# Feed-forward and perceptron of a hybrid block: the first product in turned form

## The chip, the cores and the metric

One core of a Trainium2 chip runs the whole kernel. The metric is device microseconds of one execution, the median of several runs. PE is TensorE (its weight loads are PEld), DVE VectorE, ACT ScalarE, POOL GpSimd, SP the queue that issues the loads. Line numbers (L693) are those of the kernel before.

## The reference, cut to what matters

Two blocks follow each other on 256 rows of 1,024 numbers, all in fp32. The first has two layers, each a mixer of three attentions and then a gated feed-forward. The second has two layers, each an attention and then a perceptron with squared ReLU. Only the feed-forward and the perceptron bear on the change:

```
def swiglu(h, w_ffn_in, w_ffn_out):          # twice, FFN_HIDDEN = 2816
    gu = h @ w_ffn_in
    g, u = gu[..., :FFN_HIDDEN], gu[..., FFN_HIDDEN:]
    return (jax.nn.silu(g) * u) @ w_ffn_out

def sq_relu_mlp(x, w_in, w_out):             # twice, D_FF = 4096
    return jnp.square(jax.nn.relu(x @ w_in)) @ w_out
```

Beside the first block's layers runs `mod = silu(c) @ ada_w + ada_b`, whose 12 chunks of 512 columns a layer give the scales and shifts of its norms (the modulation rows).

## The kernel before, in words

**Products in parts.** Every large product is made in fp32r with each operand split in a high part (rounded) and a low part (what is left). A weight unit is 256 rows by 512 columns, 512 KB. SP loads it into one of five raw slots, in one fixed order of all units, rows of constants and modulation weights (`stream`, made by `plan`). ACT rounds it to `hi_units` (L1112, `prep`), POOL subtracts to `lo_units` (L656), five slots each, and PE multiplies (`unit`, L693). A chunk is 512 output columns; its two row tiles of 128 are summed in a pair of PSUM banks, and chunks take the two pairs in turn.

In `unit` the activations are stationary and the weights stream past: for each row tile and each 128 rows of the contraction three passes of 512 columns, high by high, high by low weight, low activation by high weight. A unit is 12 matmuls.

**Activations.** They must lie turned, with the contraction on the partitions, high and low part beside each other (`turned`, and `turned_wide`, called AT, for the hidden numbers). `turn_ffn` (L2076) transposes a finished chunk on PE, 128 by 128 at a time, into the turning banks TQ and TP; ACT copies the rounded part to SBUF (`turn_hi_ffn`, L1140), DVE subtracts the low part (`turn_lo_ffn`, L1489).

**Feed-forward.** Six chunks j of gate (`ffg`) and of value (`ffu`), the last of 256 columns. ACT takes tanh of half the gate from the bank (L1330), DVE makes gate times sigmoid (L1914), then the product with the value into the row buffer `o_rows` (L1922). PE turns chunk j-1 after the gate product of chunk j. The last chunk is turned inside `wide`, the product with `w_ffn_out` over AT.

**Perceptron.** Eight chunks (`mi`). ACT takes ReLU into `mlp_relu` (L1363), DVE squares it, SBUF by SBUF, into `o_rows` (L2058). PE turns chunk j-1 after product j, the last one inside `wide` (product `mo`).

**First chunk.** In both, `beginning` starts chunk 0 while the norm's rows are still being turned: row tile 0 over all four units, then row tile 1.

**Modulation rows.** In the feed-forward of the first layer 32 units of modulation weights are streamed among the weights (three slots), in the second layer 8. DVE multiplies and sums each in two operations (L1431, L1434), rounds and splits a finished chunk (L1439, L1444); PE sums it over the partitions with two matmuls of 512 columns (`ada_sum`, L750, L751), and DVE adds the bias (`ada_drain`, L1455 to L1459). Each engine works its program in order. On DVE `before(key)` does the modulation units that stand in the stream up to one unit past the next chunk, and `after(key)` drains what is complete. PE's `sums()` makes the sums that come due behind a chunk.

Of the kernel before, what the change touches and what calls it, by code (L numbers as in the profile page):

```python
# [29 lines left out]
P = 128  # L30
# [116 lines left out]
def plan():  # L147
# [16 lines left out]

    def vec(name, src, col0, ncols=CW):
# [30 lines left out]
    def phase(parts, adas, summed=True, lead=0, tail=0):  # L196
# [5 lines left out]
        total = sum(-(-args[3] // UNIT_K) for _, args in parts) - lead - tail  # L202
        seen = sent = 0
        for vec_args, args in parts:
            done = []
            c = chunk(*args)
# [25 lines left out]
    for l in range(DEPTH):  # L232
# [31 lines left out]
        for j in range(-(-FFN // CW)):  # L264
            n = min(CW, FFN - j * CW)
            parts.append((None, (("ffg", l, j), ("w_ffn_in", l), 0, KT, j * CW, n)))
            parts.append((None, (("ffu", l, j), ("w_ffn_in", l), 0, KT, FFN + j * CW, n)))
# [8 lines left out]
    for i in range(2):  # L276
# [8 lines left out]
        for j in range(DFF // CW):  # L285
            put(chunk(("mi", i, j), ("mlp_w_in", i), 0, KT, j * CW, CW))
# [38 lines left out]
def program(nc, ctx, dram, out, cat, book):  # L325
# [54 lines left out]
    one_end = union + max(FFN // P * 2 * S * 4 + 2 * NT * CW * 4, NT * (PROJ_W + 3 * D) * 4)  # L380
    MOD, mod_at = place("mod_rows", [P, 6 * D], at=-(-one_end // 64) * 64)
# [174 lines left out]
    def _(sp):  # L556
        sp.dma_start(COND, dram["c"].rearrange("b (p k) -> (b p) k", p=P)).then_inc(c_in, 16)
        sp.dma_start(CON[:, 0:n_early], dram["constants"][:, 0:n_early]).then_inc(const_in, 16)
        for item in stream:
# [32 lines left out]
            else:  # L592
                src, row0, n, col0, ncols = item["src"]
                a = tile_rows(src)[row0:row0 + n * P, col0:col0 + ncols].rearrange("(k p) n -> p k n", p=P)
# [68 lines left out]
    def _(pe):  # L663
        todo = [c for c in chunks]

        def pair_free(c):
            what, i, *half = c["before"]
            if half == [1] and what in ("wo", "mo") or c["before"] == ("ffo", 1, 1):

                pe.wait_ge(vec_used.sem, vec_used.at(("final_g", 1) if what == "ffo" else ({"wo": "ln_mix_b", "mo": "ln_mlp_b"}[what], i, 1)))  # L670
                return
            if c["before"][0] == "mi":
                pe.wait_ge(act_side.sem, act_side.at(("relu", *c["before"][1:])))
            else:
                pe.wait_ge(drained.sem, drained.at(c["before"]))

        def unit(c, i, A, tiles=range(NT)):
# [20 lines left out]
            elif i == len(c["units"]) - 1:  # L698

                ins.then_inc(product.sem, product.mark(("first tile", c["key"])))  # L700

# [97 lines left out]
        def wide(tag, n, name, following):  # L799

            c = todo.pop(0)
            last = n - 1
            width = (FFN - last * CW if name == "ffo" else CW) // P
            for i in range(len(c["units"])):
                if i == 2 * last - 2:
                    turn_ffn(pe, turned, turned_lo, rows, drained, tag, last, width, BANK, TQ, TP, O, con)

                pe.wait_ge(turned_lo.sem, turned_lo.at((tag, i // 2, 1)))
# [125 lines left out]
        for l in range(DEPTH):  # L934
# [93 lines left out]
            n_ff = -(-FFN // CW)  # L1028
            for j in range(n_ff):
                if j < n_ff:  # L1030
                    for what in ("ffg", "ffu"):
                        if (what, j) != ("ffg", 0):
                            c = todo.pop(0)
                            assert c["key"] == (what, l, j)
                            for i in range(len(c["units"])):
                                unit(c, i, HT)
                        sums()
                        if what == "ffg" and j:
                            turn_ffn(pe, turned, turned_lo, rows, drained, ("a", l), j - 1, min(CW, FFN - (j - 1) * CW) // P, BANK, TQ, TP, O, con)
            wide(("a", l), n_ff, "ffo", (("n1", 1), O, n1_rows) if l + 1 < DEPTH else (("x", 0), X, x_rows(0)))  # L1040
        for i in range(2):
# [17 lines left out]
            for j in range(DFF // CW):  # L1059
                if j:  # L1060
                    c = todo.pop(0)
                    for u in range(len(c["units"])):
                        unit(c, u, HT)
                    turn_ffn(pe, turned, turned_lo, rows, drained, ("a2", i), j - 1, CW // P, BANK, TQ, TP, O, con)
            wide(("a2", i), DFF // CW, "mo", (("x", 1), X, x_rows(1)) if i == 0 else None)
# [1050 lines left out]
```

## Time and profile before

| | |
|---|---|
| median of 3 runs | 1515.95 us (1514.25 to 1517.46) |
| profiled execution: time, span | 1513.58 us, 1511.8 us |
| busy of the span | PE 97%, PEld 81%, POOL 81%, DVE 47%, ACT 47% |
| instructions | 20,262, of them 7,242 matmuls |
| HBM read | 311.39 MB |

A busy share says how long an engine had something in hand, not that it set the end; which engine does is read from the chain that ended last. Matmuls are pipelined, so the time of one is read from how often they start, not from its own duration.

### The profile page before, as it was taken

Reading aid. Unit: us, or ns where it says so; the run is one execution under the profiler, and the core shown is the slowest. Engines: PE = TensorE matmul, PEld = TensorE weight load, DVE = VectorE, ACT = ScalarE, POOL = GpSimd, SP = SyncE. Lnnn points to the kernel's source line nnn. Section 1 sums busy time; section 2 is a strip of 40 time slices with the busy share of each in tenths; the row PEclk is TensorE's granted clock in tenths of the full one; section 3 lists DMA queues with packets and bytes.
Section 4 is the critical chain, followed back from the end, with each engine's and each line's share of the span. In section 5 each row is a group of like instructions: output and inputs, shape, how many; then the busy total and the mean of one; then the engine's idle time right before and its main releaser. Section 6 shows DMA issues by size and latency. Waiting matters only on the chain.

```text
span 1511.8 us, 20262 instructions
## 1 busy us (share of the span) xinstructions
PE 1473.0 (97%) x7242; PEld 1220.8 (81%) x7242; DVE 710.6 (47%) x1398; ACT 711.8 (47%) x1074; POOL 1217.6 (81%) x984
## 2 busy tenths in 40 slices
PE   7999999999999999999999999999999999999997
PEld 3898887788888987888788887778888888788886
DVE  7577655665724668656433114264331053643212
ACT  3345554544444344545544445465554345455432
POOL 4799989798797976548898888908999977389994
PEclk9999999999999999999999999999999999999999
DMA  9995546799976985426676665715655656166553
GB/s 356 317 391 178 176 157 190 232 354 304 299 230 207 380 269 153 133 84 214 197 245 187 198 219 162 212 56 153 195 185 191 211 166 208 46 177 195 182 188 104
DMA packets 168238, 313.79 MB, mean 208 GB/s; under 512 B 11061, under 2 KB 36041, under 8 KB 168137
## 3 DMA queue, kind: packets, MB, share of 16 engines
q1 hardware_dynamic: 166384, 311.15, 64.0%
q10 hardware_dynamic: 1754, 1.35, 0.3%
q8 instruction: 58, 0.95, 0.3%
q14 instruction: 42, 0.34, 0.1%
HBM read 311.39 MB, written 1.06 MB: 207 GB/s over the span
## 4 chain that ended last, share of the span: by engine, by line
PE 86%; DVE 5%; POOL 3%; DMA 3%; ACT 2%; issue 1%; SPq 0%; DVEq 0%; ACTq 0%; POOLq 0%
PE bank L693 75%; POOL lo_units L656 3%; PE bank L2076 2%; PE bank L838 2%; PE bank L859 1%; DMA raw_units<-in_w_in 1%; ACT hi_units L1112 1%; PE bank L827 1%; PE bank L826 1%; PE bank L877 1%; PE bank L825 1%; DMA row_vectors<-in_norm_g 1%; DMA raw_units<-in_w_out 1%; PE bank L725 1%; PE bank L862 0%
## 5 line engine op out<-in xcount | busy, mean ns | idle before, releaser
L656 POOL TENSOR_TENSOR lo_units<-raw_units,hi_units 128x512 fp32r<-128x512 f32 (+3 forms) x944 | 1167.7, 1275 | 258.9 <-ACT hi_units L1112 257.3
L693 PE MATMUL bank<-hi_units,turned 128*128 128x512 f32 (+2 forms) x2688 | 832.6, 385 | 4.6 <-POOL lo_units L656 3.0
L1112 ACT ACTIVATE hi_units<-raw_units 128x1024 fp32r<-128x1024 f32 (+3 forms) x478 | 485.5, 1018 | 535.4 <-PE bank L693 428.4
L693 PEld LDWEIGHTS bank<-hi_units,turned 128*128 128x128 f32 x2688 | 501.6, 189 | 98.9 <-POOL lo_units L656 4.3
L693 PE MATMUL bank<-lo_units,turned 128*128 128x512 f32 (+3 forms) x1344 | 511.6, 381 | 0.0
L693 PE MATMUL bank<-hi_units,turned_wide 128*128 128x512 f32 x992 | 311.0, 391 | 0.9 <-DVE turned_wide L1482 0.9
L693 PEld LDWEIGHTS bank<-lo_units,turned 128*128 128x128 f32 x1344 | 253.8, 189 | 41.9 <-issue 0.2
L693 PEld LDWEIGHTS bank<-hi_units,turned_wide 128*128 128x128 f32 x992 | 186.2, 188 | 39.9 <-DVE turned_wide L1482 1.1
L693 PE MATMUL bank<-lo_units,turned_wide 128*128 128x512 f32 x496 | 193.1, 389 | 0.0
L1434 DVE SCALAR_TENSOR_TENSOR bank<-ada_units,small,bank 128x512 f32<-128x512 f32 x144 | 108.8, 756 | 54.0 <-DMA ada_units<-in_ada_w 49.7
L693 PEld LDWEIGHTS bank<-lo_units,turned_wide 128*128 128x128 f32 x496 | 93.2, 188 | 19.0 <-issue 0.2
L2058 DVE TENSOR_TENSOR o_rows<-mlp_relu 128x512 f32<-128x512 f32 x32 | 47.1, 1510 | 116.2 <-ACT mlp_relu L1363 116.2
L1489 DVE TENSOR_TENSOR turned_wide<-bank,turned_wide 128x512 fp32r<-128x512 f32 (+1 forms) x56 | 37.7, 672 | 93.2 <-ACT turned_wide L1140 91.4
L1227 ACT ACTIVATE scores<-scores,small 128x128 f32<-128x128 f32 x60 | 24.0, 400 | 57.8 <-DVE small L1649 57.2
L1914 DVE SCALAR_TENSOR_TENSOR ffn_tanh<-ffn_tanh,bank 128x512 f32<-128x512 f32 (+1 forms) x24 | 14.3, 639 | 70.1 <-ACT ffn_tanh L1330 70.0
L1951 DVE SCALAR_TENSOR_TENSOR bank<-x_rows,bank 128x512 f32<-128x512 f32 x8 | 5.6, 696 | 75.8 <-PE bank L693 75.6
L838 PE MATMUL bank<-constants,scores 128*128 128x128 f32 x180 | 31.1, 282 | 4.9 <-DVE o_rows L1667 1.9
L693 PE MATMUL bank<-hi_units,branch_turned 128*128 128x512 f32 x96 | 32.8, 403 | 0.0
L1667 DVE TENSOR_TENSOR o_rows<-bank,small 128x128 f32<-128x128 f32 x48 | 14.0, 292 | 37.6 <-PE bank L827 36.6
L1922 DVE SCALAR_TENSOR_TENSOR o_rows<-ffn_tanh,bank 128x512 f32<-128x512 f32 (+1 forms) x24 | 14.3, 639 | 35.0 <-PE bank L693 34.9
L1146 ACT ACTIVATE turned<-bank 128x512 fp32r<-128x512 f32 x28 | 16.8, 599 | 27.7 <-PE bank L725 27.7
L1229 ACT ACTIVATE scores<-scores,small 128x256 f32<-128x256 f32 x60 | 29.7, 494 | 0.0
(235 smaller groups left out, 1238.1 us busy)
## 6 DMA issues: line engine op xcount, KB each, us to landing
ada_units<-in_ada_w SPq DMA_DIRECT2D x88, 512.0 KB, 7.6
raw_units<-in_w_ffn_in SPq DMA_DIRECT2D x80, 512.0 KB, 4.5
raw_units<-in_mlp_w_in SPq DMA_DIRECT2D x64, 512.0 KB, 4.0
raw_units<-in_mlp_w_out SPq DMA_DIRECT2D x64, 512.0 KB, 3.3
raw_units<-in_w_in SPq DMA_DIRECT2D x56, 458.0 KB, 7.6
raw_units<-in_w_in SPq DMA_DIRECT2D x48, 512.0 KB, 3.9
raw_units<-in_w_ffn_out SPq DMA_DIRECT2D x44, 512.0 KB, 4.1
raw_units<-in_moba_w_qkv SPq DMA_DIRECT2D x24, 512.0 KB, 4.1
```

Source lines behind the costliest of these rows:

```text
L656: pool.tensor_tensor(LO[:, s, b, 0:w], RAW[:, u["slot"], b, 0:w], HI_[:, s, b, 0:w].bitcast(F32), ALU.subtract).then_inc(lo_ready.sem, lo_ ...
L693: ins = pe.matmul(BANK[2 * c["pair"] + t][:, 0:w], xs[:, part, :], W[:, s, b, 0:w], start=(i == 0 and m == 0 and q == 0), stop=(i == len(c ...
L725: ins = pe.transpose(BANK[(TQ, TP)[n % 2]][:, j * P:(j + 1) * P], src[:, t, (4 * half + j) * P:(4 * half + j + 1) * P], con("ident"))
L838: ins = pe.transpose(bank[:, at:at + P], SM[:, h % N_SM, cols], con("ident"))
L1112: act.activation(HI_[:, s, 0:n, 0:w], RAW[:, u["slot"], 0:n, 0:w], ACT.Copy)\
L1146: act.activation(A[:, 4 * half:4 * half + 4, 0, t * P:(t + 1) * P], BANK[(TQ, TP)[n % 2]][:, :].rearrange("p (k s) -> p k s", k=4), ACT.Copy)\
L1227: act.activation(SM[:, h % N_SM, S:S + P], SM[:, h % N_SM, S:S + P], ACT.Exp, bias=NM[:, m:m + 1], scale=-1.0, accum_out=RS[:, m:m + 1])
L1229: act.activation(SM[:, h % N_SM, 0:S], SM[:, h % N_SM, 0:S], ACT.Exp, bias=NM[:, m + 1:m + 2], scale=-1.0, accum_out=RS[:, m + 1:m + 2]).t ...
L1434: ins = v.scalar_tensor_tensor(total, raw[:, k, :], COND[:, kt:kt + 1], partial, ALU.mult, ALU.add)
L1489: tell(v.tensor_tensor(AT[:, 4 * j:4 * j + n, 1, t * P:(t + 1) * P], BANK[(TQ, TP)[t]][:, 0:n * P].rearrange("p (k s) -> p k s", k=n), AT[ ...
L2058: ins = v.tensor_tensor(O[:, t, (j % 2) * CW:(j % 2 + 1) * CW], RT[:, j % 2, t, :], RT[:, j % 2, t, :], ALU.mult)
L2076: ins = pe.transpose(BANK[(TQ, TP)[t]][:, k * P:(k + 1) * P], O[:, t, (j % 2) * CW + k * P:(j % 2) * CW + (k + 1) * P], con("ident"))
```

## The change

Chunk 0 of gate and value, and chunk 0 of the perceptron, stay as they are. All later hidden columns are made in tiles of 128 columns in turned form: the weights are stationary and the activations stream past, high and low part side by side in 512 columns, then the low weight over the 256 columns of the high activations. What comes out has the hidden columns on the partitions, and its two halves of 256 have to be added. A unit is now the 1,024 rows of one tile; the weights come from copies laid out in such tiles (`w_ffn_tiles`, `mlp_w_tiles`, made before the launch), 4 KB in a row. A feed-forward has 18 such tiles of gate and value (36 units, keys `fft`), a perceptron 28 tiles (two in a chunk, keys `mit`).

DVE adds the two halves (`both_parts`, a reduction over a view with stride 256) from the product's bank into the first 256 columns of a turning bank. Gate, tanh, ReLU, square and the splitting then work there and write AT directly. Only chunk 0 is transposed, between the two units of the first turned chunk. The plan spreads the modulation units over 2 units a turned chunk. The core of the diff:

```
+        def tile_free(c, i):
+            what, l, n = c["before"]
+            if what == "mit":
+                pe.wait_ge(rows.sem, rows.at(("sum", l, n + i)))
+            elif what == "fft" and i == 0:
+                pe.wait_ge(rows.sem, rows.at(("gate tile", l, n)))
+            elif what == "fft":
+                pe.wait_ge(drained.sem, drained.at(c["before"]))
+            elif i == 0:
+                pair_free(c)
+
+        def turned_unit(c, i, A):
+            u = c["units"][i]
+            tile_free(c, i)
+            s = u["index"] % NH
+            bank = BANK[2 * c["pair"] + i]
+            for kt in range(KT):
+                b, at = divmod(kt * P, CW)
+                if at == 0:
+                    pe.wait_ge(lo_ready.sem, lo_ready.at((u["index"], b)))
+                pe.matmul(bank[:, :], HI_[:, s, b, at:at + P], A[:, kt, :, :].rearrange("p two s -> p (two s)"), start=kt == 0, stop=False)
+                ins = pe.matmul(bank[:, 0:S], LO[:, s, b, at:at + P], A[:, kt, 0, :], start=False, stop=kt == KT - 1)
+            ins.then_inc(unit_used.sem, unit_used.mark(u["index"]))
+
+        def turned_product(key, between=None):
+            c = todo.pop(0)
+            turned_unit(c, 0, HT)
+            if between:
+                between()
+            turned_unit(c, 1, HT)
...
-                pe.wait_ge(turned_lo.sem, turned_lo.at((tag, i // 2, 1)))
+                pe.wait_ge(turned_lo.sem, turned_lo.at((tag, 0, 1) if i < CW // P // 2 else (tag, "tile", 2 * i + 1)))
                 unit(c, i, AT)
...
+            for n in range(CW // P, FFN // P):
+                turned_product(("fft", l, n), first_turn if n == CW // P else None)
+                sums()
...
+            for n in range(CW // P, DFF // P, 2):
+                turned_product(("mit", i, n), first_turn if n == CW // P else None)
```

ACT, in the feed-forward and in the perceptron:

```
+        def hidden_hi(tag, n, h):
+            act.wait_ge(rows.sem, rows.at((tag, "hidden", n)))
+            act.activation(AT[:, n, 0, :], h, ACT.Copy).then_inc(turned_hi.sem, turned_hi.mark((tag, "hidden", n)))
...
+            for n in range(CW // P, FFN // P):
+                prep_chunk(("fft", l, n), NH - 1)
+                if n == CW // P:
+                    turn_hi_ffn(("a", l), 0, CW // P)
+                act.wait_ge(rows.sem, rows.at(("gate tile", l, n)))
+                act.activation(TGN[:, n % 2, 0, :], BANK[TQ][:, 0:S], ACT.Tanh, scale=0.5)\
+                    .then_inc(act_side.sem, act_side.mark(("tg", l, n)))
+                prep_chunk(("fft", l, n))
+                hidden_hi(("a", l), n, BANK[TP][:, 0:S])
...
+                for m in (n, n + 1):
+                    act.wait_ge(rows.sem, rows.at(("sum", i, m)))
+                    act.activation(RTN[:, m % 4, :], BANK[(TQ, TP)[m % 2]][:, 0:S], ACT.Relu).then_inc(act_side.sem, act_side.mark(("relu tile", i, m)))
+                    prep_chunk(("mit", i, n), NH - 1 if m == n else NH)
+                    hidden_hi(("a2", i), m, BANK[(TQ, TP)[m % 2]][:, 0:S])
```

DVE, in the same order:

```
+        def hidden_lo(tag, n, h):
+            dve.wait_ge(turned_hi.sem, turned_hi.at((tag, "hidden", n)))
+            tell(v.tensor_tensor(AT[:, n, 1, :], h, AT[:, n, 0, :].bitcast(F32), ALU.subtract), turned_lo, (tag, "tile", n))
+
+        def both_parts(to, bank):
+            return v.tensor_reduce(to, bank[:, :].rearrange("p (two s) -> p s two", two=2), AX_X, ALU.add)
...
+            for n in range(CW // P, FFN // P):
+                key = ("fft", l, n)
+                tg, g, u = TGN[:, n % 2, 0, :], BANK[TQ][:, 0:S], BANK[TP][:, 0:S]
+                if n == CW // P:
+                    turn_lo_ffn(("a", l), 0, CW // P)
+                say(both_parts(g, tile_product(dve, key, 0)), ("gate tile", l, n))
+                if n > CW // P:
+                    hidden_lo(("a", l), n - 1, u)
+                if n < FFN // P - 1:
+                    before(key)
+                dve.wait_ge(act_side.sem, act_side.at(("tg", l, n)))
+                link(v.scalar_tensor_tensor(tg, tg, 1.0, g, ALU.add, ALU.mult))
+                tell(both_parts(u, tile_product(dve, key, 1)), drained, key)
+                say(v.scalar_tensor_tensor(u, tg, 0.5, u, ALU.mult, ALU.mult), (("a", l), "hidden", n))
+                after(key)
...
+                for m in (n, n + 1):
+                    h = BANK[(TQ, TP)[m % 2]][:, 0:S]
+                    if m == CW // P:
+                        turn_lo_ffn(("a2", i), 0, CW // P)
+                    say(both_parts(h, tile_product(dve, key, m - n)), ("sum", i, m))
+                    if m > CW // P:
+                        hidden_lo(("a2", i), m - 1, BANK[(TQ, TP)[(m - 1) % 2]][:, 0:S])
+                    dve.wait_ge(act_side.sem, act_side.at(("relu tile", i, m)))
+                    say(v.tensor_tensor(h, RTN[:, m % 4, :], h, ALU.mult), (("a2", i), "hidden", m))
```

`tile_product` waits for one unit and gives its bank; TGN and RTN are 256-column views of the tanh and ReLU buffers.

## Rows read from the trace of the kernel before

**Rows 1.** The page: busy shares, the chain's shares, products of L693 (group rows).

```profile
PE 1473.0 (97%) x7242; PEld 1220.8 (81%) x7242; DVE 710.6 (47%) x1398; ACT 711.8 (47%) x1074; POOL 1217.6 (81%) x984
...
PE 86%; DVE 5%; POOL 3%; DMA 3%; ACT 2%; issue 1%; SPq 0%; DVEq 0%; ACTq 0%; POOLq 0%
PE bank L693 75%; POOL lo_units L656 3%; PE bank L2076 2%; PE bank L838 2%; PE bank L859 1%; DMA raw_units<-in_w_in 1%; ACT hi_units L1112 1%; PE bank L827 1%; PE bank L826 1%; PE bank L877 1%; PE bank L825 1%; DMA row_vectors<-in_norm_g 1%; DMA raw_units<-in_w_out 1%; PE bank L725 1%; PE bank L862 0%
...
L693 PE MATMUL bank<-hi_units,turned 128*128 128x512 f32 (+2 forms) x2688 | 832.6, 385 | 4.6 <-POOL lo_units L656 3.0
...
L693 PEld LDWEIGHTS bank<-hi_units,turned 128*128 128x128 f32 x2688 | 501.6, 189 | 98.9 <-POOL lo_units L656 4.3
```

**Rows 2.** Chain in order of time, first perceptron: start us, us, what.

```profile
1060.41 0.87 PE bank L2076 x8
1061.29 10.90 PE bank L693 x48
1072.19 0.87 PE bank L2076 x8
...
1131.93 32.66 PE bank L693 x144
```

**Rows 3.** The same view, first feed-forward.

```profile
289.60 27.25 PE bank L693 x120
316.85 0.23 PE bank L750
...
405.98 5.75 PE bank L693 x48
...
434.00 0.44 PE bank L2076 x4
```

**Rows 4.** Timeline of ACT and DVE around chunk 0: start us, us, instruction.

```profile
306.09 1.28 DVE L1922 SCALAR_TENSOR_TENSOR o_rows<-ffn_tanh,bank 128x512 f32<-128x512 f32 x2 [1.40 <-PE bank L693]
...
1049.63 1.06 ACT L1112 ACTIVATE hi_units<-raw_units 128x1024 fp32r<-128x1024 f32 x1 [0.30 <-PE bank L693]
1050.60 1.07 ACT L1363 ACTIVATE mlp_relu<-bank 128x512 f32<-128x512 f32 x2
...
1051.77 3.45 DVE L2058 TENSOR_TENSOR o_rows<-mlp_relu 128x512 f32<-128x512 f32 x2 [6.29 <-ACT mlp_relu L1363]
...
1074.41 2.61 DVE L2058 TENSOR_TENSOR o_rows<-mlp_relu 128x512 f32<-128x512 f32 x2 [6.85 <-ACT mlp_relu L1363]
...
1335.48 3.45 DVE L2058 TENSOR_TENSOR o_rows<-mlp_relu 128x512 f32<-128x512 f32 x2 [6.33 <-ACT mlp_relu L1363]
```

**Rows 5.** Timeline of POOL, end of the first perceptron's chunks.

```profile
1120.52 2.99 POOL L656 TENSOR_TENSOR lo_units<-raw_units,hi_units 128x512 fp32r<-128x512 f32 x2 [0.19 <-ACT hi_units L1112]
...
1144.06 2.54 POOL L656 TENSOR_TENSOR lo_units<-raw_units,hi_units 128x512 fp32r<-128x512 f32 x2 [0.18 <-ACT hi_units L1112]
```

**Rows 6.** Busy time in one stretch, first feed-forward: us, engines, PEclk, DMA, GB/s.

```profile
289.00:412.00 123.00, 123.00 (x611) 104.29 (x610) 80.29 (x114) 58.63 (x71) 107.92 (x93) 1.00 0.92 311
```

**Rows 7.** Groups by form on DVE in the same stretch, modulation rows.

```profile
L1434 DVE SCALAR_TENSOR_TENSOR bank<-ada_units,small,bank 128x512 f32<-128x512 f32 x51 | 38.5, 756 | 7.8 <-DMA ada_units<-in_ada_w 6.1
...
L1459 DVE SCALAR_TENSOR_TENSOR mod_rows<-bank,row_vectors 128x512 f32<-128x512 f32 x2 | 1.4, 692 | 0.1
```

**Rows 8.** Groups by form, whole span, DVE and ACT.

```profile
L1504 DVE TENSOR_TENSOR bank<-x_rows,mod_rows 128x512 f32<-128x512 f32 x6 | 6.8, 1175 | 0.1
...
L1953 DVE BATCH_NORM_STATS2 small<-bank 128x6 f32<-128x512 f32 x8 | 5.6, 699 | 0.3
...
L1489 DVE TENSOR_TENSOR turned_wide<-bank,turned_wide 128x256 fp32r<-128x256 f32 x4 | 1.7, 426 | 33.4 <-ACT turned_wide L1140 33.3
...
L1112 ACT ACTIVATE hi_units<-raw_units 128x1024 fp32r<-128x1024 f32 x382 | 404.0, 1059 | 407.1 <-PE bank L693 383.9 <-DMA raw_units<-in_w_out 7.9 <-DMA raw_units<-in_w_ffn_out 7.5
...
L1140 ACT ACTIVATE turned_wide<-bank 128x256 fp32r<-128x256 f32 x4 | 1.3, 370 | 0.0
```

**Rows 9.** Waits in the first feed-forward: us in total, times, longest us.

```profile
ACT hi_units L1112 <- DMA raw_units<-in_w_ffn_in: 2.4, 1, 2.4
```

More of the change, by code:

```diff
@@ L163, in chunk, with tile_chunk @@
         return c
+    def tile_chunk(key, tiles):
+        c = dict(key=key, kind="gemm", pair=pair[0] % 2, ncols=CW, units=[])
+        pair[0] += 1
+        for name, l, n in tiles:
+            c["units"].append(dict(kind="w", index=count["w"], n=UNIT_K, ncols=CW, src=("tiles", name, l, n)))
+            count["w"] += 1
+        chunks.append(c)
+        return c
     def vec(name, src, col0, ncols=CW):
@@ L201, in phase @@
         made = {}
-        total = sum(-(-args[3] // UNIT_K) for _, args in parts) - lead - tail
+        total = sum(2 if args[0][0] == "fft" else -(-args[3] // UNIT_K) for _, args in parts) - lead - tail
         seen = sent = 0
@@ L671, in pair_free @@
                 return
+            if what == "mit":
+                pe.wait_ge(rows.sem, rows.at(("sum", i, half[0] + 1)))
+                return
             if c["before"][0] == "mi":
@@ L1027, in _ @@
             beginning(("n2", l), O, n2_rows, HT)
[L1028 to L1040, printed above, removed]
+            c = todo.pop(0)
+            assert c["key"] == ("ffu", l, 0)
+            for i in range(len(c["units"])):
+                unit(c, i, HT)
+            sums()
+            first_turn = lambda l=l: turn_ffn(pe, turned, turned_lo, rows, drained, ("a", l), 0, CW // P, BANK, TQ, TP, O, con)
+            for n in range(CW // P, FFN // P):
+                turned_product(("fft", l, n), first_turn if n == CW // P else None)
+                sums()
+            wide(("a", l), (("n1", 1), O, n1_rows) if l + 1 < DEPTH else (("x", 0), X, x_rows(0)))
         for i in range(2):
@@ L1058, in _ @@
             beginning(("m", i), X, m_rows, HT)
[L1059 to L1065, printed above, removed]
+            first_turn = lambda i=i: turn_ffn(pe, turned, turned_lo, rows, drained, ("a2", i), 0, CW // P, BANK, TQ, TP, O, con)
+            for n in range(CW // P, DFF // P, 2):
+                turned_product(("mit", i, n), first_turn if n == CW // P else None)
+            wide(("a2", i), (("x", 1), X, x_rows(1)) if i == 0 else None)
         assert not todo
@@ L1925, in _ @@
[L1925 removed]
+            kg, ku = ("ffg", l, 0), ("ffu", l, 0)
+            before(kg)
+            banks = product_ready(dve, kg)
+            dve.wait_ge(act_side.sem, act_side.at(("tg", l, 0)))
+            for t in range(NT):
+                ins = v.scalar_tensor_tensor(TG[:, 0, t, :], TG[:, 0, t, :], 1.0, banks[t][:, :], ALU.add, ALU.mult)
+            tell(ins, drained, kg)
+            after(kg)
+            before(ku)
+            banks = product_ready(dve, ku)
@@ L2101, in traced, with in_tiles @@
     return nc
+def in_tiles(inputs):
+    out = {}
+    for name, to in (("w_ffn_in", "w_ffn_tiles"), ("mlp_w_in_2", "mlp_w_tiles_2")):
+        w = np.asarray(inputs[name])
+        tiles = w.reshape(w.shape[0], KT, P, -1, P).transpose(0, 3, 2, 1, 4)
+        out[f"in_{to}"] = np.ascontiguousarray(tiles).reshape(w.shape[0], -1, P, D)
+    return out
 def kernel(**inputs):
```

125 lines of the change are left out of this document (51 added, 74 removed).

## The prediction

> **What bounds the kernel now.** I read the page's busy shares first: PE holds 97% of the span and nothing else comes near except POOL at 81% [rows 1]. The chain that ended last confirms that this is work and not a coincidence of busy engines: PE carries 86% of it, the products of L693 alone 75%, and the transposes of L2076 2% [rows 1]. So time falls only if PE streams less or waits less, and any other engine costs nothing until it makes PE wait. I then read the chain in order of time, in one perceptron [rows 2] and in the first feed-forward [rows 3]: product, transposes, product, with no gap between them. Four units take 10.90 us, a group of eight transposes 0.87 us. The granted clock is full in these stretches (1.00, that is 2.4 GHz, in the first feed-forward [rows 6]), so I take durations as they stand.
>
> **Part 1, the transposes that go.** A perceptron has eight groups of eight transposes; seven go. The group takes 0.87 us [rows 2], so 2 x 7 x 0.87 = 12.2 us. A feed-forward has five groups of eight and one of four (0.44 us [rows 3]); four of eight and the one of four go: 2 x (4 x 0.87 + 0.44) = 7.8 us. They lie on the chain itself, so all 20.0 us come off PE.
>
> **Part 2, the product in turned form.** A unit was 12 matmuls of 512 columns: 10.90 / 4 = 2.725 us, or 227 ns for one with its weight load beside it. It becomes 8 matmuls of 512 and 8 of 256 columns, the same 6,144 columns in 16 pieces. For a 256-column one there is a row: the half-width chunk of the feed-forward, 48 in 5.75 us, 120 ns each, every one with a 128-column load of its own [rows 3]. So a turned unit costs 8 x 0.227 + 8 x 0.120 = 2.775 us. Perceptron: 28 units a layer, 28 x 0.05 = 1.4 us more. Feed-forward: before, 32 full units and 8 half ones (5.75 / 4 = 1.44 us), 87.2 + 11.5 = 98.7 us; after, 36 x 2.775 = 99.9, 1.2 us more. Both layers of both: +5.2 us. Bounds: without the extra four fixed parts (227 ns less 213 ns of columns, 14 ns each) it would be +0.0 to +0.5; from above, a load's own record lasts 189 ns [rows 1]; if a short matmul couldn't run under it, each of the 1,024 short ones would take 69 ns more, 70 us in all. The half-width chunk has the same loads (loads and matmuls stand in equal numbers) and runs at 120 ns, so I keep 120 and leave that end to rival D. The rule that speaks for that end is the Trainium skill's "TensorE: Matmul & The Clock Gate", section "LDWEIGHTS (loading the stationary operand)": a load takes its columns over 1.2 GHz, by estimate 107 ns for 128, what 256 columns take at 2.4 GHz, so nothing would be to spare. By that rule the trace agrees in the half-width chunk, 107 ns of columns and 120 ns measured, so the sum would be the same.
>
> **Part 3, the turn of the first chunk moves forward.** Only chunk 0 is still transposed, and now between the two units of the first turned product, one unit (2.775 us) after chunk 0 ends; before, a whole chunk (10.9 us) lay between. What must be ready is the squares or the gated rows in the row buffer.
> In the perceptron ACT's conversion at 1049.63 starts as chunk 0's last unit ends (about 1049.5); ReLU runs from 1050.60 and the two squares of L2058 from 1051.77 to 1055.22 [rows 4]. So the rows are ready 5.8 us after the chunk, and PE, with 2.775 us of work, stands 3.0 us; the other perceptron shows the same 3.45 us pair [rows 4]. 2 x 3.0 = +6.0 us. Queued behind the wait are the transposes and all later units; ACT's next conversions wait behind the turn too, but they have about four units (11 us) of lead. Bounds: the same pair took 2.61 us once [rows 4], so 2 x 2.2 = 4.4; above, 7.5 if ACT is late by another conversion (1.06 us less a semaphore). The pair is this slow against 1.28 us for a gating pair [rows 4] since both its inputs lie in SBUF while POOL reads there too: POOL's unit takes 2.99 us beside it and 2.54 us otherwise [rows 5]. The new operations all have an input in PSUM, as the gating pair has, so I charge POOL nothing for them.
> In the feed-forward DVE's gating of chunk 0 ran 306.09 to 307.37 [rows 4], 1.4 us after the chunk ended near 305.95: inside one unit, no stall.
>
> **Part 4, what DVE, ACT and POOL get.** Per turned tile of 128 hidden columns. DVE: a sum of two halves of a bank. No such reduction stands in the trace; it reads 512 elements of PSUM, and its nearest rows, statistics over a bank and the drain of one, take 0.69 to 0.70 us [rows 7, 8]. I take 0.69. Lower bound 0.43 us (a 256-element operation, since it writes 256 [rows 8]); upper 1.18 us, the slowest 512-element form that touches PSUM [rows 8]. Low part, gate and product over 256 go by the low part of the old half chunk, 0.42 us each [rows 8].
> Perceptron, per unit of 2.775 us: DVE 0.69 + 2 x 0.42 = 1.5 us; ACT one conversion 1.06 and two 256-wide passes of 0.37 [rows 8], 1.8 us; POOL 2.54 us [rows 5]. All fit, hidden by PE's 2.775 us; POOL has the least to spare, 0.23 us, and were it slower by more than that, PE would follow it (2.85 us a unit would be 56 x 0.075 = 4 us). Against that, in the wide products PE already runs 144 matmuls in 32.66 us, 2.72 a unit, over the same POOL work [rows 2].
> The first feed-forward is the tight one. DVE has the modulation rows there: 59.7 us for 29.5 of its units in 123 us (seven rows, the first and the last shown) [rows 7], 2.02 us each, 2.1 with gaps. By the plan 27 of 32 are streamed by the end of the turned tiles, 4 are done before, so 23: 48.7 us. Gating and splitting 18 tiles: 18 x (2 x 0.69 + 3 x 0.42 + gaps 0.18) = 50.7 us. First turn 1.4 and waiting for it 2.5. Together 103.3 us. PE in the same stretch: 99.9 + 0.87 + six modulation sums of 0.46 [rows 3] = 103.5 us. DVE is as full as PE. What softens it: PE needs a sum only two tiles later (three units, 8.3 us) and a finished modulation row about 5 us after DVE can start it. So a lag under 5 us is free. I charge 1.0 us; bounds 0 and, with the sum at 1.18 us, 36 x 0.49 - 5 = 12.6 us. In the second feed-forward only 8 modulation units come: nothing.
> DMA moves the same bytes, in rows of 4 KB in place of 2 KB; the queue's weights landed in time (ACT waited 2.4 us for them in that stretch, once [rows 9], and PE didn't wait: busy 123 of 123 us [rows 6]). 0. The moved place of the next waits (the wide product needs tile 5 at its third unit, the last tile at its last) is far behind the work: 0.
>
> **Sum.** -20.0 + 5.2 + 6.0 + 1.0 = -7.8 us. On the profiled execution: 1513.6 (span 1511.8) to 1505.8. The median shown is 2.4 us above that execution, so 1515.95 - 7.8 = 1508.1, 0.5% faster. A measurement here tells about 0.2%, 3.0 us.
>
> **Rivals.**
> A. The stalls are small: pairs of squares at 2.61 us and no loss on DVE: -20.0 + 5.2 + 4.4 = -10.4, 1505.6. For it: the 2.61 us pair. Against: both first pairs took 3.45.
> B. DVE's lag in the first feed-forward grows beyond its 5 us, by in-order waits for tanh and for modulation transfers (DVE waited 6.1 us for the latter in this stretch before [rows 7]): 4 to 8 us lost, -5 to -1, 1511 to 1515. Against: each look-ahead for transfers is now shorter, two units in place of four.
> C. The other side: the sum over the halves takes about 1.2 us. DVE then needs 36 x 0.49 = 17.6 us more in the first feed-forward, 12.6 beyond the lag: -20.0 + 5.2 + 6.0 + 12.6 = +3.8, 1519.7. It decides from 0.69 + (8.8 + 5) / 36 = 1.07 us per sum. For it: the 1.18 us row, and no row of a reduction. Against: every form with one PSUM input and no second SBUF input takes 0.69 to 0.76 us.
> D. Short matmuls bound by their loads: 70 us at the full 69 ns, 1578; it decides the sign from 8 ns each (1,024 x 0.008 = 8 us). The half-width row speaks against it.
>
> **Chances.** Forecast (1506.5 to 1510) 0.50, A and anything better 0.18, B 0.18, C 0.10, D 0.04. Faster by over 0.2% (below 1512.9): forecast, A and a third of B, 0.74. Within 0.2%: the rest of B and a little of C, 0.14. Slower: 0.12. The range leaves out D, half of C and the best of A: 1503.5 to 1518.
>
> **What would show it.** Right: four turned units of one stage 11.1 us apart on the chain; 32 transposes of L2076's kind in place of 216; PE idle 3 us in the first turned product of each perceptron, released by the squares; reductions at 0.69 us; POOL at 2.54 us a unit all through the perceptron. Wrong: PE waiting in the first feed-forward for DVE's sums or its modulation rows; a sum over 1 us; 256-column matmuls more than 120 ns apart; POOL over 2.77 us a unit, which would make it the bound.

## The result, and the profile after

The changed kernel takes 1523.28 us (median of 6 runs, 1520.28 to 1525.83) against 1515.47 us (1513.47 to 1517.46, 6 runs) before: ratio 1.0049, interval [1.0034, 1.0065]. It is slower by 7.8 us where 7.8 us less were forecast. The profiled execution took 1525.83 us (span 1524.0), the slowest of the six, so its span stands 12.2 us above that of before and not 7.8.

The page after (busy shares, then the chain's shares by engine):

```profile
PE 1470.8 (97%) x7474; PEld 1225.8 (80%) x7474; DVE 798.1 (52%) x1630; ACT 718.1 (47%) x1154; POOL 1206.8 (79%) x968
...
PE 73%; DMA 7%; DVE 7%; POOL 7%; ACT 3%; issue 1%; SPq 0%; DVEq 0%; ACTq 0%
```

PE's share of the chain fell from 86% to 73%, while its busy share stayed at 97% [rows 1]. Most of the 13% went to DMA, POOL and DVE: somewhere the kernel waits for them. To see where, I cut both traces at the last four transposes that turn a norm's output, which stand at the head of each stage (us from there to the next, or to the end):

| stage | before | after | difference |
|---|---|---|---|
| first feed-forward | 191.5 | 200.3 | +8.8 |
| attention of layer 2 | 248.9 | 249.2 | +0.3 |
| second feed-forward | 189.5 | 188.7 | -0.8 |
| first perceptron | 184.2 | 186.8 | +2.7 |
| second perceptron | 184.7 | 184.3 | -0.3 |

The rest of the 12.2 us is 1.4 us ahead of the first feed-forward and 0.2 us in the two attentions of the second block, where the code is the same. No changed stage gained what its transposes took (3.9 or 6.1 us), and one lost 9.

**New operations.** Groups by form, whole span (count, busy us, mean ns, idle before):

```profile
L746 PE MATMUL bank<-turned,hi_units 128*128 128x512 f32 x1024 | 363.6, 400 | 0.2 <-DVE bank L1557 0.2
...
L747 PE MATMUL bank<-turned,lo_units 128*128 128x256 f32 x1024 | 287.7, 281 | 0.0
...
L1557 DVE TENSOR_REDUCE bank<-bank 128x256 f32<-128x512 f32 x128 | 89.5, 700 | 94.9 <-PE bank L747 93.3
```

The sum over two halves takes 700 ns, for which 0.69 had been taken. A matmul's own duration overlaps the next; its true cost is read from the starts, in the next view.

**First perceptron, chain in order of time.**

```profile
1059.23 1.06 ACT hi_units L1165
1060.29 0.98 ACT mlp_relu L1416 x2
...
1061.36 3.44 DVE o_rows L2128 x2
...
1064.84 1.97 PE bank L2155 x8
1066.81 0.43 PE bank L746
1067.24 0.21 PE bank L747
1067.45 0.43 PE bank L746
...
1071.90 0.24 PE bank L746
...
1072.96 0.24 PE bank L746
```

Conversion, ReLU, squares, then the transposes, as foreseen, with PE idle 2.9 us. Not foreseen is what follows: the eight transposes take 1.97 us where 0.87 is usual [rows 2], and a long and a short matmul take 0.64 us (1066.81 to 1067.45). From 1071.90 on three pairs take 1.06 us, 0.353 each. The windows over PE (us busy, granted clock, DMA share, GB/s) say why:

```profile
1060.00:1064.00 4.00, 1.94 (x12) 1.00 0.75 249
1064.00:1068.00 4.00, 3.16 (x13) 0.52 0.41 135
1068.00:1072.00 4.00, 4.00 (x17) 0.63 0.37 131
1351.00:1355.00 4.00, 3.49 (x15) 0.59 0.48 142
```

Behind the wait the granted clock stands at 0.50, the 1.2 GHz level, until 1071.0; some 6 us of PE's work fall in it. The fourth row is the same place in the second perceptron, where the low stretch is half as long. Its length isn't given by the stall: with the same early turn the low stretch behind it in the first perceptron is as long in e4_mlp_only (6.9 us), and half as long (3.4 us) in e2_half_mod, e3_grouped and e11_paced_only.

The pace of a pair is not one number either. From the second perceptron, on the same chain:

```profile
1385.11 0.23 PE bank L746
...
1386.15 0.23 PE bank L746
```

Three pairs take 1.04 us, 0.347 each, at the same clock of 1.00. So the units of the second perceptron start 2.77 us apart, while those of the second feed-forward and the first perceptron start 2.83 us apart. As long as units follow each other without an interruption they keep one of the two paces; behind a wait or a modulation sum it can change, as it does within the first feed-forward.

**First feed-forward, one stretch** (columns as in [rows 6]), and under it the waits in it, of the engines and then of SP's queue (us in total, times, longest). The last fence has the queue's waits for DVE in the same stretch of the kernel before:

```profile
300.00:425.00 125.00, 121.29 (x665) 103.93 (x664) 103.88 (x167) 54.80 (x80) 104.35 (x84) 1.00 0.83 290
```

```profile
ACT hi_units L1165 <- DMA raw_units<-in_w_ffn_tiles: 35.1, 18, 4.7
...
DVE ffn_tanh L1996 <- ACT ffn_tanh L1390: 7.3, 6, 3.1
```

```profile
SPq L604 <- DVE bank L1491: 46.2, 15, 8.6
SPq L604 <- DVE sum_low L1501: 28.7, 6, 7.5
SPq L619 <- POOL lo_units L674: 11.2, 13, 2.2
```

```profile
SPq L591 <- DVE sum_low L1444: 7.1, 5, 2.5
SPq L591 <- DVE bank L1434: 2.6, 4, 1.7
```

PE is no longer busy throughout. ACT, which waited once for weights before [rows 9], waits 18 times, 35.1 us. Yet the DMA engines are busy only 0.83 of the time (0.92 before [rows 6]): the transfers are issued late. SP issues them in one fixed order, and now stands 75 us (9.7 before) at L604, a modulation load, until DVE frees one of the three slots; every weight load behind it in the queue stands too. The chain shows a whole turn of this, at the end of the tiles:

```profile
415.99 5.30 DMA raw_units<-in_w_ffn_out
...
421.32 0.03 ACT hi_units L1165
...
422.28 0.38 ACT turned_wide L1199
...
422.75 0.44 DVE turned_wide L1553
...
425.52 0.70 DVE sum_low L1501
...
426.24 0.37 SPq L604
...
426.65 6.08 DMA raw_units<-in_w_ffn_out
...
432.76 1.07 ACT hi_units L1165
...
433.89 2.52 POOL lo_units L674 x2
...
436.45 14.68 PE bank L714 x57
```

Weights land late; ACT's small pass on the hidden tile is queued behind their conversion; DVE waits for that pass, with the modulation unit queued behind; the slot is freed late; SP issues the next weights 10 us after the last ones. This is a ring of waits: each step is late by the one before it, and the last one makes the first late again. The start of the output product pays for it: in the tiles PE is idle 3.7 us, behind them another 3, with a stretch at the lower clock.

### The profile page after: what moved, and what is told of

The parts are those of the page before. It is cut to its first block, busy times and chain, and to the rows that moved or that the text cites. A ratio compares the mean times of both kernels' runs of the same rounds, so it can differ in the third digit from the quotient of the medians.

```text
span 1524.0 us, 21278 instructions
## 1 busy us (share of the span) xinstructions
PE 1470.8 (97%) x7474; PEld 1225.8 (80%) x7474; DVE 798.1 (52%) x1630; ACT 718.1 (47%) x1154; POOL 1206.8 (79%) x968
## 3 DMA queue, kind: packets, MB, share of 16 engines
HBM read 311.39 MB, written 1.06 MB: 205 GB/s over the span
## 4 chain that ended last, share of the span: by engine, by line
PE 73%; DMA 7%; DVE 7%; POOL 7%; ACT 3%; issue 1%; SPq 0%; DVEq 0%; ACTq 0%
PE bank L714 47%; PE bank L746 11%; POOL lo_units L674 7%; PE bank L747 6%; DMA ada_units<-in_ada_w 3%; DMA raw_units<-in_w_ffn_tiles 2%; PE bank L891 1%; ACT hi_units L1165 1%; PE bank L912 1%; DVE bank L1491 1%; DMA raw_units<-in_w_ffn_out 1%; DMA raw_units<-in_w_in 1%; PE bank L880 1%; PE bank L879 1%; PE bank L930 1%
## 5 line engine op out<-in xcount | busy, mean ns | idle before, releaser
L1165 ACT ACTIVATE hi_units<-raw_units 128x1024 fp32r<-128x1024 f32 (+1 forms) x470 | 483.2, 1031 | 431.1 <-PE bank L714 225.0
L714 PE MATMUL bank<-hi_units,turned 128*128 128x512 f32 (+3 forms) x1600 | 508.3, 389 | 4.6 <-POOL lo_units L674 3.0
L746 PE MATMUL bank<-turned,hi_units 128*128 128x512 f32 x1024 | 363.6, 400 | 0.2 <-DVE bank L1557 0.2
L714 PEld LDWEIGHTS bank<-hi_units,turned 128*128 128x128 f32 x1600 | 301.4, 189 | 62.1 <-POOL lo_units L674 4.3
L714 PE MATMUL bank<-lo_units,turned 128*128 128x512 f32 (+3 forms) x800 | 306.7, 383 | 0.0
L747 PE MATMUL bank<-turned,lo_units 128*128 128x256 f32 x1024 | 287.7, 281 | 0.0
L746 PEld LDWEIGHTS bank<-turned,hi_units 128*128 128x128 f32 x1024 | 193.6, 189 | 47.6 <-DVE bank L1557 0.5
L747 PEld LDWEIGHTS bank<-turned,lo_units 128*128 128x128 f32 x1024 | 194.5, 190 | 0.5
L714 PEld LDWEIGHTS bank<-lo_units,turned 128*128 128x128 f32 x800 | 151.5, 189 | 23.9 <-issue 0.2
L1557 DVE TENSOR_REDUCE bank<-bank 128x256 f32<-128x512 f32 x128 | 89.5, 700 | 94.9 <-PE bank L747 93.3
```

The source lines that it names most:

```text
L714: ins = pe.matmul(BANK[2 * c["pair"] + t][:, 0:w], xs[:, part, :], W[:, s, b, 0:w], start=(i == 0 and m == 0 and q == 0), stop=(i == len(c ...
L746: pe.matmul(bank[:, :], HI_[:, s, b, at:at + P], A[:, kt, :, :].rearrange("p two s -> p (two s)"), start=kt == 0, stop=False)
L747: ins = pe.matmul(bank[:, 0:S], LO[:, s, b, at:at + P], A[:, kt, 0, :], start=False, stop=kt == KT - 1)
L1165: act.activation(HI_[:, s, 0:n, 0:w], RAW[:, u["slot"], 0:n, 0:w], ACT.Copy)\
L1557: return v.tensor_reduce(to, bank[:, :].rearrange("p (two s) -> p s two", two=2), AX_X, ALU.add)
```

## The experiments

Stage times are those of the profiled execution of each kernel; medians are over all its runs. Each kernel was timed beside runs of the kernel before, whose median was 1515.3 to 1516.2 us throughout.

**1. The turn behind both units of the first turned chunk, in the perceptrons alone** (e1_late_turn).

```
             turned_unit(c, 0, HT)
-            if between:
+            if between and not late:          # late: the perceptrons
                 between()
             turned_unit(c, 1, HT)
+            if between and late:
+                between()
```

> The changed kernel, only that in the two perceptrons the turn of chunk 0 comes after both units of the first turned chunk, not between them. Theory: PE stands about 3 us in each perceptron for the squares, and in the first one its clock then falls (matmul pairs 640 ns apart for about 3 us), so two units (5.65 us) under a wait of 5.8 us leave 0.2 us: 6 to 9 us less than the changed kernel (1523.3), 1514 to 1517. Rival: the perceptron is paced by POOL or by DVE's sums, and the wait only moves: within 1.5 us of 1523.3.

1516.09 us, ratio 1.0002 [0.9991, 1.0012], 7.2 us less than the changed kernel; the perceptrons take 181.2 and 180.3 us in place of 186.8 and 184.3. Its chain at the same place:

```profile
1059.81 3.48 DVE o_rows L2131 x2
...
1063.33 1.09 PE bank L2158 x8
1064.43 0.23 PE bank L746
```

**2. PE kept at work through the wait** (e8_filled): the changed kernel with 12 matmuls, read by nobody, between the first unit and the turn.

> The changed kernel, with 12 matmuls of 512 columns, whose product nobody reads, between the first turned unit and the turn of each perceptron's first chunk: 12 x 227 ns = 2.7 us, so that TensorE works through the wait for the squares instead of standing idle. It saves no waiting. Theory (the idle 2.9 us is followed by a stretch at the lower clock, which costs 3.4 us in the first perceptron and 1 to 2 in the second): the granted clock stays at 1.00 behind the turn, the eight transposes take 0.9 us, the pairs 353 ns, and the kernel 3 to 5 us less than the changed one, 1518 to 1520. Rival (the clock falls for another reason, or the stretch is slow because the bank's readers are in the way): transposes still take 2 us, pairs 640 ns, and the time stays at 1523.

1520.87 us (10 runs), ratio 1.0034 [1.0022, 1.0045]: 2.4 us less than the changed kernel, just short of the 3 to 5 expected. The perceptrons take 184.0 and 183.1 us. The windows over PE:

```profile
1064.00:1068.00 4.00, 3.86 (x25) 1.00 0.52 150
1068.00:1072.00 4.00, 4.00 (x25) 1.00 0.29 113
```

The clock stays full although the wait is as long. So the stall of 2.9 us had two prices in the profiled execution: itself, and 2.8 us (first perceptron) and 1.2 us (second) at the low clock. The Trainium skill, "TensorE: Matmul & The Clock Gate", section "What's actually happening", says that the clock's gate follows how busy the array has recently been; by that rule the trace agrees.

The second price isn't paid each time. In e11_paced_only (below), with the same early turn, the second perceptron has the same stall (2.9 us idle in these two rows) and no fall:

```profile
1334.00:1338.00 4.00, 1.42 (x9) 1.00 0.60 215
1338.00:1342.00 4.00, 3.70 (x24) 1.00 0.51 161
```

That fits the medians, where keeping PE at work gave 2.4 us and not 4.0. What decides whether the clock falls behind a wait of this length, and for how long, no run here shows.

**3. Long matmuls first, then the short ones** (e3_grouped, on the changed kernel; e6_late_grouped, on e1_late_turn).

```
             for kt in range(KT):
                 (long matmul)
+            for kt in range(KT):
                 (short matmul)
```

> The changed kernel, each turned unit with its eight 512-column matmuls first and its eight 256-column ones behind them. In the changed kernel a pair takes 353 ns where rows of equal length give 227 + 120 = 347. Theory: the change of length after each matmul costs the 6 ns, and grouping takes 128 x 8 x 6 ns = 6 us off PE; of it 3 to 4 us are seen (the first feed-forward waits for DVE anyway): 1519 to 1521. Rival: the operands' places cost it, whatever the order: within 1.5 us of 1523.3.

> Late turn as in e1_late_turn, and the eight long matmuls of a turned unit ahead of its eight short ones. Theory (a part of the 353 ns that a pair takes, above 227 + 120, comes from the alternation of lengths): a unit takes 2.78 to 2.80 us in place of 2.83, the second feed-forward 187.2 us in place of 188.2, each perceptron 1 us less than in e1_late_turn, so 1512 to 1514. Rival (it belongs to the lengths, not to their order): 1516, as e1_late_turn.

e3_grouped: 1522.2 us, ratio 1.0041 [1.0025, 1.0057]; e6_late_grouped: 1515.22 us, 0.9989 [0.9979, 1.0000]. Each is about 1 us below its base, within the intervals, and above the range expected of it; the 1522.2 us lie in the rival's range. The starts of the units say more. Grouped units start 2.79 us apart in all four stages of both kernels, wherever nothing comes between. Alternating ones start 2.83 or 2.77 us apart, so grouping gains where they held the slower pace (second feed-forward 187.4 us against 188.7 in the changed kernel; first perceptron 180.4 against 181.2 in e1_late_turn) and loses where they held the faster one (second perceptron 180.8 against 180.3). So the 6 ns above 227 + 120 belong to the alternation, but only to one of its two paces; at the other it costs nothing. Why there are two is open.

**4. The first feed-forward apart.** e4_mlp_only has both feed-forwards as before the change and the perceptrons as after it.

> Both feed-forwards as before the change, both perceptrons as after it. By the stages of the two traces the feed-forwards account for 8.0 us of the loss (8.8 in the first, -0.8 in the second) and the perceptrons for 2.3 us (2.6 and -0.3). Theory: 1516 to 1518. Rival, the loss lies in the perceptrons: 1521 to 1524.

1517.46 us, 1.0007 [0.9995, 1.0018], first feed-forward back at 191.5 us. e7_first_ffn_old has only the first one as before, with late turn and grouped matmuls in the rest.

> Late turn, grouped matmuls, and the first feed-forward as before the change; the second feed-forward and both perceptrons in turned form. Theory: stages of 191.5 us (first feed-forward, as before the change), 187.2 (second), 180.5 and 179.5 (perceptrons), which is 2 + 3.7 + 5.2 us less than before the change in the three changed stages: 1503 to 1508. Rival (what the second feed-forward and the perceptrons save is only moved to a later wait): 1512 to 1516.

1505.14 us (5 runs), ratio 0.9932 [0.9917, 0.9947]; stages 191.5, 187.4, 180.4 and 180.8 us. The turned form is worth its transposes in three stages of four.

**5. Less work on DVE.** e2_half_mod is the changed kernel without the second multiplication of each modulation unit in the first feed-forward (these sums are half left out). e5_three_short keeps all work, but spares DVE the sum over halves.

```
-    (long: W_hi x [A_hi A_lo] -> bank[:, 0:512]), (short: W_lo x A_hi -> bank[:, 0:256])
+    (short: W_hi x A_hi), (short: W_hi x A_lo), (short: W_lo x A_hi), all -> bank[:, 0:256]
```

> The changed kernel, but DVE leaves out the second of the two multiplications of every modulation unit streamed in the first layer's feed-forward (half of those sums is missing from the result); all transfers stay. DVE gets about 18 us lighter there, DMA stays as it is. Theory: DVE is overfull in that stage and holds back both the modulation slots, behind which the weights queue, and the tanh and split steps: PE's waits there go, about 9 us less than the changed kernel, 1513 to 1516. Rival: the transfers themselves are too slow (HBM rate, 4 KB rows): within 1.5 us of 1523.3.

> The turn of the perceptron's first chunk stands behind both units, as in e1_late_turn. Besides, in the first feed-forward alone each pair of a long and a short matmul becomes three short ones into columns 0 to 255 of the bank, so that VectorE copies 256 numbers where it had to add two halves (700 ns each, 36 of them in that stage). Theory (VectorE is overfull in the first feed-forward and its lateness reaches TensorE through the slots of the modulation's raw columns): VectorE gets back some 10 us there, at 0.35 to 0.4 us less for each of 36 sums 12 to 14 us, while TensorE pays 8 x (3 x 120 - 353) ns = 0.06 us a unit, about 2 us in all; the stage comes from 199.9 us to 193 to 196, the whole to 1508 to 1513. Rival (the transfers of that stage are late by themselves, since tile by tile weights come in another order): the stage stays at 199 to 202 us and the whole at 1516 to 1519.

e2_half_mod: 1517.68 us, 1.0013 [1.0000, 1.0026], 5.6 less than the changed kernel (about 9 expected), stage 192.7. e5_three_short: 1510.77 us, 0.9970 [0.9961, 0.9979], within its range, but its stage took 198.7, above the 193 to 196 expected. The window over the tiles, of e2_half_mod and then of e5_three_short:

```profile
300.00:425.00 125.00, 125.00 (x685) 107.67 (x684) 88.25 (x146) 56.44 (x82) 108.16 (x87) 1.00 0.84 301
```

```profile
300.00:425.00 125.00, 125.00 (x964) 121.41 (x963) 97.29 (x172) 54.39 (x79) 106.06 (x85) 1.00 0.82 290
```

In both PE works through, with every transfer where it was, so DVE has a part in the loss within the tiles, and the bytes alone don't make it. But e5_three_short still lost 3.2 us at the start of the output product, and the clock fell there. The theory as I had it, DVE simply overfull, was not enough.

**6. The same work, transfers spread wider.** The plan places one modulation unit for each 1.5 weight units. Here a turned tile's unit counts 0.7 (e9_paced) or 0.8 (e10_paced_08) and the last ones of the output product count too, so that 24 or 25 of 32 are streamed by the end of the tiles and not 27.

```
-                seen += 1
+                seen += share if args[0][0] == "fft" else 1
```

> All four stages in turned form, late turn and grouped matmuls as in e6_late_grouped. Besides, the plan spreads the 32 modulation units of the first feed-forward otherwise: a unit of a turned tile counts 0.7 and not 1, and the last half unit of the first output product counts too, so that 23 and no longer 27 of them are streamed by the end of the tiles; the rest lies beside the output product. Nothing is left out. Theory (VectorE is overfull in the tiles, and four modulation units less are 4 x 2.1 = 8.4 us of its 103): TensorE no longer waits there, the stage takes 190 to 194 us in place of 201.7, the whole 1504 to 1508. Rival (the first transfers of the output product's weights are late anyway, as in e5_three_short, where VectorE had 10 us less and the stage still took 198.6 us): 196 to 199 us, the whole 1510 to 1513.

> As e9_paced with 0.8 in place of 0.7: 25 of the 32 modulation units by the end of the tiles. Theory: VectorE has 4.2 us less, half of what e9_paced gives, so the stage takes 194 to 198 us and the whole 1508 to 1511; were it the same as e9_paced, VectorE's fullness would not be what counts but the place of the transfers. Rival: no change to e6_late_grouped, 1515.

e9_paced: 1506.39 us, 0.9933 [0.9910, 0.9956], stage 192.0. e10_paced_08: 1505.36 us, 0.9926 [0.9905, 0.9947], stage 191.3, better than expected. (The expectation counts 23 units for e9_paced; in the order in which SP issues them it is 24, counted as the 27 and the 25 are.) Two units moved out of 27 gave back all of the 10 us, and three gave no more. By its expectation that speaks against DVE's load and for the place of the transfers. The waits of e10_paced_08 in the stretch 300:425:

```profile
SPq L604 <- DVE bank L1496: 52.9, 17, 7.6
SPq L604 <- DVE sum_low L1506: 23.7, 7, 5.7
```

```profile
ACT hi_units L1170 <- DMA raw_units<-in_w_ffn_tiles: 21.0, 10, 3.9
...
DVE ffn_tanh L2001 <- ACT ffn_tanh L1395: 0.2, 1, 0.2
```

SP stands for DVE as long as in the changed kernel, 76.6 us for 75, and nothing is lost: the sum of the queue's waits doesn't tell whether they do harm. What fell is ACT's wait for the tiles' weights (35.1 to 21.0) and DVE's for tanh (7.3 to 0.2). e11_paced_only made the same edit on the changed kernel itself.

> The changed kernel with nothing but the other spread of the modulation units (a tile's unit counts 0.8): early turn and alternating matmuls stay. Theory (the first feed-forward's loss is independent of the perceptrons'): the first feed-forward takes 191 to 193 us in place of 200.3, and the whole 1513 to 1516; the perceptrons keep their stall and the lower clock behind it. Rival (the spread works only together with the grouped matmuls, which leave TensorE ready earlier or VectorE later): 1518 to 1523.

1516.31 us (10 runs), 1.0002 [0.9993, 1.0012], just above its range; stage 192.6, perceptrons 185.2 and 184.5: the two losses are independent.

**7. DVE's load put back.** In e10_paced_08 the gate's sum over halves is made twice, in every third tile (e12_paced_extra_sums, +4.2 us) or in every tile (e14_every_sum_twice, +12.6 us).

> e10_paced_08 with VectorE's load put back and the transfers left where they are: in the first feed-forward the sum over the two halves of the gate's bank is made twice in every third tile, 6 x 0.70 = 4.2 us, as much as the two modulation units that e10_paced_08 moved out. Nothing is left out. Theory A (VectorE's fullness in the tiles decides): the loss comes back, the stage takes 196 to 202 us and the whole 1510 to 1515. Theory B (what helped was where the modulation transfers stand among the weights in SyncE's queue): the stage stays at 191 to 192 us and the whole at 1505 to 1506.

> e10_paced_08 with the gate's sum over two halves made twice in all 18 tiles of the first feed-forward: 18 x 0.70 = 12.6 us more on VectorE, three times the dose of e12_paced_extra_sums. Nothing is left out. Theory (a circle of waits, which needs late transfers to close, but VectorE has under 10% to spare): the stage takes 195 to 203 us, since VectorE now truly has more work, some 112 us, than TensorE's 104; the whole 1508 to 1517. Rival (VectorE's load does not matter at all as long as the transfers are spread): 191 to 192 us, 1504 to 1506.

e12_paced_extra_sums: 1503.68 us (4 runs), 0.9911 [0.9886, 0.9936], stage 191.6. e14_every_sum_twice: 1513.08 us (10 runs), 0.9981 [0.9971, 0.9990], stage 198.3. Windows of the two:

```profile
300.00:425.00 125.00, 125.00 (x689) 108.73 (x689) 111.18 (x177) 55.15 (x80) 107.93 (x86) 1.00 0.86 299
```

```profile
300.00:425.00 125.00, 120.72 (x666) 104.75 (x665) 111.95 (x179) 56.62 (x82) 104.76 (x84) 1.00 0.84 287
```

DVE at 111.2 us of 125 does no harm, at 7 us more than the changed kernel had in the stretch where it lost. So its busy time by itself was not the cause; it is a bound too, but farther up: with the triple dose PE waits for its modulation sums (4.3 us here). The load was put back as sums ahead of the tanh and not as modulation units, so this tests how much DVE does, and not where in its order.

**8. The ring cut at one place** (e16_tanh_first): transfers as in the changed kernel, but ACT converts one unit fewer ahead of each tanh.

```
-                prep_chunk(("fft", l, n), NH - 1)
+                prep_chunk(("fft", l, n), NH - (2 if l == 0 else 1))
                 ...
                 act.activation(TGN[...], BANK[TQ][:, 0:S], ACT.Tanh, scale=0.5)
```

> e6_late_grouped (transfers as in the changed kernel) with one edit in the first feed-forward: ScalarE converts one weight unit fewer ahead of each tile's tanh (and that unit right after it), so that tanh does not queue behind a conversion whose weights have not landed. Theory (a circle through the slots, SyncE's queue, ScalarE's conversions, tanh and VectorE): cut here, VectorE's waits for tanh, 5 to 7 us, go, the stage falls from 201.7 to between 191 and 196 us and the whole from 1515 to 1505 to 1510. Rival (VectorE's own work and the place of the transfers make the lateness, tanh is a symptom): 199 to 202 us and 1514 to 1516.

1510.89 us (6 runs), 0.9964 [0.9951, 0.9978]: 4.3 us less than e6_late_grouped, from which it differs by this line; stage 196.1 against 201.8, the whole just above its range.

```profile
300.00:425.00 125.00, 125.00 (x689) 108.78 (x688) 107.84 (x172) 56.16 (x79) 106.44 (x85) 1.00 0.86 296
```

DVE's waits for tanh (6.7 us in e6_late_grouped's first feed-forward) are gone and PE works through the tiles, with no operation less anywhere. What stays, about 5 us, is at the output product, where the chain of this run has the ring of above once more, through ACT's pass on the hidden tile, which this edit leaves behind the conversions. That pass was not moved in any run, and no run gave the modulation loads a queue or a slot of their own, so the links through that pass and through SP's queue are read from the chain and not tested by themselves. So the lateness is carried, in the part that this edit removed by experiment and in the rest as the chain shows it, by the order in the queues of SP, ACT and DVE. The Trainium skill, "TensorE: Matmul & The Clock Gate", section "Architectural detail: the array is 16× 32×32, not 1× 128×128", says that ACT and DVE are strictly first in, first out; the chain agrees (the pass at 422.28 starts behind the conversion at 421.32).

## Why the prediction was wrong, point by point

**Part 1, right.** Of 216 transposes 32 are left, four groups of eight. In the undisturbed second feed-forward 3.9 us of transposes less and 36 units at 2.83 us (101.9 less the old 98.7, +3.2) make -0.7; measured -0.8.

**Part 2, right in kind, mis-sized.** 2.775 us was forecast for a unit. The 28 units of the second perceptron take 2.77, the other 100 about 2.83 (a pair 353 ns): 100 x 0.055 = 5.5 us more, so +10.7 for +5.2. The two prices of 227 and 120 ns were each read from a run of equal matmuls, and whether a stage would keep their sum could not be read from the trace of before. The lower bound was also off: without the extra fixed parts a unit costs 2.725 us as before, and the feed-forwards with 36 units (98.1 us against 98.7) bring the term to -1.2, not +0.0.

**Part 3, the wait right, its price half.** PE stood 2.9 us in each perceptron, released by the squares, as forecast (3.0). The sum took the wait for the whole price, while I had read all durations at the full clock. The clock's fall added 4.0 us in the two perceptrons of the profiled execution, 2.4 by the medians. The early turn costs 7.2 us by e1_late_turn; one unit later it leaves no wait that the trace shows.

**Part 4, the failed step: "a lag under 5 us is free", with 1.0 us charged.** The sizes were right: the sum 0.70 us, POOL 2.54 us a unit, DVE busy 103.9 us of the 125 shown. The loss was 9.5 us (+8.8 against the -0.7 of an undisturbed stage). I asked how long PE can do without DVE, and not who else waits for it: SP for the slots, in a queue that carries the weights. I took the queue at 0 since its weights had landed in time before and the bytes stay the same. Rival B named the in-order waits for tanh and for modulation transfers, at 4 to 8 us; it had the right place and links, but not SP's queue; the price was too low, and what I held against it (a shorter look-ahead) did not hold. Rival C did not occur, nor D, though its sign, 256-column matmuls more than 120 ns apart, was there by 6 ns a pair in three stages.

With the measured terms: -20.0 + 10.7 + 5.8 + 4.0 + 9.5 = +10.0 us, for +10.4 in the four changed stages; the parts with the same code add 1.9 us, which together make up the 12.2 between the two spans. The second perceptron closes too: -6.1 + 1.3 + 2.9 + 1.2 = -0.7, and it took -0.3. The medians differ by 7.8 only. The profiled execution has the longer low stretch in the first perceptron, which other runs had half as long, and 1.4 us ahead of the first feed-forward; further than that the difference isn't traced. Why two modulation units suffice (e10_paced_08), and whether one would, was not measured.

The change pays with three edits that undo nothing of it, late turn, grouped matmuls and wider spread: 1505.36 us (e10_paced_08), where the kernel before took 1515.25 beside it. It can't be told from e7_first_ffn_old (1505.14), or from e12_paced_extra_sums, which does more work.

## What to carry to other kernels

Where one queue issues loads of two kinds in a fixed order, a consumer that frees slots of the one kind late also delays the other: before moving work to an engine, follow who waits for its slots. That SP's queue begins to wait for it is a reason to look, not a measure of the loss: here it stood 75 us with the loss and 76.6 without. A stall of PE can be charged with the clock behind it, so put work ahead of the wait, as the late turn does. Read the pace of a stage in each stage: the same code held two. A busy share does not tell a full engine from one that is part of a ring of waits: putting the load back and cutting one link did.

## What was not expected of the hardware

A wait of 2.9 us was followed by some 6 us of work at half the granted clock in the first perceptron, by a shorter stretch in the second, and by none in the second perceptron of e11_paced_only; 12 matmuls in the wait kept it at 1.00. Alternating 512- and 256-column matmuls took 353 or 347 ns a pair at the same clock, each pace held from unit to unit until something came between; eight and eight took 349 (2.79 us a unit) throughout, and three of 256 took 360 (24 in 2.88 us in e5_three_short). The reduction over two halves of a bank in PSUM, read with a stride of 256, took 700 ns, no more than a plain pass over the bank.
